# Mixture-of-experts weight ring: one whole matrix per slot instead of half matrices of two experts, a separate gather for the second pair, and the last matrices in quarters

## The reference, cut to what matters

```python
gate = p_grp * p_in / jnp.sum(p_in, axis=-1, keepdims=True)      # weights of the token's two experts
expert = grp[:, None] * MOE_PER_GROUP + top_i                    # their numbers, 0..31
...
def expert_block(args):                                          # the tokens of one expert
    x_blk, e = args
    return (jax.nn.silu(x_blk @ w_gate[e]) * (x_blk @ w_up[e])) @ w_down[e]
...
y = jax.ops.segment_sum(yb.astype(f32) * slot_w[:, None], slot_tok, num_segments=T + 1)[:T]
```

## Time and profile before

| | |
|---|---|
| median of 3 runs | 1164.86 us (1161.91 to 1165.02) |
| the profiled execution, its own time | 1167.04 us |
| its span in the trace | 1165.3 us |
| TensorE busy | 1062.5 us, 91% |
| VectorE busy | 399.1 us, 34% |
| ScalarE busy | 169.0 us, 15% |
| read from HBM | 300.47 MB |

### The profile page before, as it was taken

How to read it: one execution, slowest core, us unless ns; L and a number is a source line. 1 busy time by engine, 2 the same in 40 slices (tenths; PEclk the granted TensorE clock), 3 DMA queues, 4 the chain that set the end, 5 groups by cost and what they waited for, 6 DMA issues and landing times.

```text
span 1165.3 us, 15871 instructions
## 1 busy us (share of the span) xinstructions
PE 1062.5 (91%) x6537; PEld 588.5 (51%) x6537; DVE 399.1 (34%) x753; ACT 169.0 (15%) x361; POOL 29.7 (3%) x88
## 2 busy tenths in 40 slices
PE   5999989798999999989977979999989988898886
PEld 4777877537666666468655363333323322222222
DVE  3857642404222222330024155352323222222221
ACT  1131330301000000010045010100100100000001
POOL 5400000000000000000000000000000000000000
PEclk9999965798999999999989979999999999899999
DMA  9442000064766666654420257999999999999993
GB/s 358 179 149 74 3 2 0 9 280 178 303 276 273 277 275 276 286 224 156 167 104 1 85 204 289 368 420 420 420 419 420 420 420 421 419 420 421 420 422 125
DMA packets 39801, 302.50 MB, mean 260 GB/s; under 512 B 7578, under 2 KB 7736, under 8 KB 8632
## 3 DMA queue, kind: packets, MB, share of 16 engines
q1 hardware_dynamic: 38268, 301.29, 63.4%
q10 hardware_dynamic: 1468, 0.24, 0.1%
HBM read 300.47 MB, written 1.05 MB: 259 GB/s over the span
## 4 chain that ended last, share of the span: by engine, by line
PE 64%; SPq 23%; DVE 6%; DMA 3%; ACT 2%; issue 2%; DVEq 0%
SPq L528 22%; PE PS L1035 11%; PE PS L1610 10%; PE PS L1405 9%; PE PS L1419 9%; PE PS L1030 8%; DMA slot<-in_moe_w_up_dram 2%; PE PS L1592 2%; PE PS L1262 2%; PE PS L1567 1%; PE PS L1204 1%; PE PS L1251 1%; PE PS L1510 1%; SPq L551 1%; DVE AR L2050 1%
## 5 line engine op out<-in xcount | busy, mean ns | idle before, releaser
L1610 PE MATMUL PS<-slot,ATT 128*32 128x512 f32 (+1 forms) x1184 | 139.6, 609 | 24.5 <-DMA slot<-in_moe_w_up_dram 13.3
L1405 PE MATMUL PS<-XH,slot 128*128 128x256 f32 x512 | 111.6, 379 | 0.0
L1419 PE MATMUL PS<-slot,AR 128*128 128x512 f32 x256 | 111.2, 592 | 0.0
L1405 PEld LDWEIGHTS PS<-XH,slot 128*128 128x128 f32 x512 | 97.3, 190 | 16.2 <-issue 3.4
L1610 PEld LDWEIGHTS PS<-slot,ATT 128*32 128x32 f32 (+1 forms) x1184 | 40.1, 113 | 122.8 <-issue 106.8
L1030 PE MATMUL PS<-XH,slot 128*128 128x256 f32 x432 | 97.2, 389 | 3.5 <-DVE XH L1731 2.5
L1030 PEld LDWEIGHTS PS<-XH,slot 128*128 128x128 f32 x432 | 84.1, 195 | 16.1 <-DVE XH L1731 2.7
L1610 PE MATMUL PS<-AR,ATT 128*32 128x512 f32 (+1 forms) x608 | 71.8, 593 | 7.1 <-DMA AR<-in_moe_w_gate_dram 4.4
L1419 PEld LDWEIGHTS PS<-slot,AR 128*128 128x128 f32 x256 | 48.6, 190 | 58.2 <-issue 57.9
L1610 PE MATMUL PS<-slot,MASKS 128*32 128x512 f32 (+1 forms) x608 | 70.8, 594 | 1.0 <-DVE AR L2266 1.0
L1035 PE MATMUL PS<-slot,XH 128*128 128x256 f32 (+4 forms) x224 | 70.8, 475 | 0.0
(11 more groups left out here) (405 smaller groups left out, 992.7 us busy)
## 6 DMA issues: line engine op xcount, KB each, us to landing
slot<-in_moe_w_up_dram SPq DMA_DIRECT2D x40, 1024.0 KB, 25.6
slot<-in_moe_w_down_dram SPq DMA_DIRECT2D x40, 1024.0 KB, 25.6
slot<-in_moe_w_gate_dram SPq DMA_DIRECT2D x36, 1024.0 KB, 25.1
slot<-in_w_ffn_dram SPq DMA_DIRECT2D x16, 2048.0 KB, 9.8
AR<-in_ada_w_dram SPq DMA_DIRECT2D x16, 1536.0 KB, 11.2
AR<-in_moe_w_gate_dram SPq DMA_DIRECT2D x22, 1024.0 KB, 24.2
AR<-in_moe_w_up_dram SPq DMA_DIRECT2D x18, 1024.0 KB, 25.6
AR<-in_moe_w_down_dram SPq DMA_DIRECT2D x18, 1024.0 KB, 26.0
```

What stands on the lines that cost most here:

```text
L1405: ins = pe.matmul(PS[:, 2 * j + f // 2, (f % 2) * T:(f % 2 + 1) * T], slots[s][:, c * 512 + f * P:c * 512 + (f + 1) * P], HT[:, c, :], sta ...
L1419: ins = pe.matmul(PS[:, 4 + 2 * i + n, :], AT[:, j, f * T + i * P:f * T + (i + 1) * P], slots[s][:, f * D + n * 512:f * D + (n + 1) * 512] ...
L1610: ins = pe.matmul(PS[r0:r1, bank_, :], src[:, r0:r1], w[:, k * HALF + at:k * HALF + at + 512], start=start, stop=stop)
```

## The change

**Units.** A unit is now one whole matrix of one expert: one transfer of 2 MiB with 16 KiB per partition (`matrix`, `ring`). Units 0 and 1 are the gate matrices of the two experts of pair 0, 2 and 3 the up matrices, 4 and 5 the down matrices. TensorE waits for both units of a kind (`matrices`) and releases both at the end of the whole product. `WHICH` replaces `SIDE` and holds expert numbers.

**Gathers.** Pair 1 gets its tokens by a second `first_gather`, placed behind the up product of pair 0 (`own_selection`, `own_tokens`). The wide gather comes later in two parts: chunks 0 to 3 behind the up product of pair 1, chunks 4 to 7 behind its down product. Only pair 2 is the first to take its tokens from `HSS`. The loop of TensorE is now pairs 2 to 11 in two rounds of five; pairs 12 to 15 are written out.

**The last pair.** The scatter products of pair 14 stand ahead of the up product of pair 15. Its two down matrices come in eight transfers of 512 KiB, in quarters of the hidden dimension, with 4 KiB per partition. The down product takes a quarter at a time, and VectorE scales the first 512 output columns while TensorE makes the second (`down_first`, `yb_first`).

`YB`, the scaled output, moves to another buffer. The list of the experts with more tokens than fit loses its pair and side numbers.

The core of the diff:

```diff
-            def ring(u, g=0, sides=(0, 1)):
-                kind, half = u % UP // 2, u % 2
-                for k in range(2):
-                    sp.dma_start(RING[u % NR][:, k * HALF:(k + 1) * HALF], pair_side(kind, half, PERIOD * g + u // UP, sides[k]))\
-                        .then_inc(ring_loaded[u % NR], 16)
+            def matrix(kind, e):
+                return kinds[kind][bass.ds(e, 1)].rearrange("e p n -> p (e n)")
+            def ring(u, e):
+                sp.dma_start(RING[u % NR], matrix(u % UP // 2, e)).then_inc(ring_loaded[u % NR], 16)
...
-                sp.wait_ge(sems[released[before % UP]], PERIOD * g + before // UP + 1)
+                sp.wait_ge(sems[released[before % UP // 2]], PERIOD * g + before // UP + 1)
...
+            for f in range(4):
+                for k in range(2):
+                    sp.dma_start(RING[4 + k][:, f * D:(f + 1) * D], matrix(2, experts[k])[:, f * D:(f + 1) * D])\
+                        .then_inc(part_loaded[f], 16)
...
             pe.wait_ge(sems["first_low"], 1)
-            project(0, 0, 0, ("gate_half", "gate_filled"), EQUAL)
-            project(0, 0, 1, ("up_half", "up_filled"), EQUAL)
-            pe.wait_ge(sems["sels_ready"], 1)
-            gather()
+            w = matrices(0, 0, 0)
+            project(w, 0, EQUAL, (0, 4))
+            pe.wait_ge(sems["hs_ready"], 1)
+            project(w, 0, EQUAL, (4, KC)).then_inc(sems["gate_filled"], 1)
+            project(matrices(0, 0, 1), 1, EQUAL).then_inc(sems["up_filled"], 1)
+            pe.wait_ge(sems["sel_ready"], 2)
+            first_gather()
             pe.wait_ge(sems["am_ready"], 1)
             turn_hidden(4)
             pe.wait_ge(sems["selw_ready"], 1)
             turn_weights()
-            pe.wait_ge(sems["hss_filled"], KC)
+            w = matrices(0, 0, 2)
+            pe.wait_ge(sems["first_low"], 2)
+            pe.wait_ge(sems["hs_ready"], 2)
             pe.wait_ge(sems["ac_ready"], 1)
-            project_back(0, 0, EQUAL)
+            project_back(w, EQUAL).then_inc(sems["down_filled"], 1)
...
+            pair_in(0, 1)
+            pe.wait_ge(sems["sels_ready"], 1)
+            gather(0, 4)
+            pair_turn(0, 1)
+            pe.wait_ge(sems["hss_filled"], 4)
+            pair_out(0, 1)
+            pe.wait_ge(sems["yb_ready"], 2)
+            gather(4, KC)
...
+            pe.wait_ge(sems["hss_filled"], KC)
...
+            project(matrices(g, i, 0), 0, SKEWED).then_inc(sems["gate_filled"], 1)
+            pe.wait_ge(sems["yb_ready"], m)
+            pe.wait_ge(sems["gt_ready"], m)
             scatter(0)
-            scatter(1).then_inc(sems["x_done"], 1)
+            scatter(1)
+            project(matrices(g, i, 1), 1, SKEWED).then_inc(sems["up_filled"], 1)
+            pe.wait_ge(sems["selw_ready"], m + 1)
+            pe.wait_ge(sems["am_ready"], m + 1)
+            turn_hidden(4)
+            turn_weights()
...
+            for f in range(4):
+                pe.wait_ge(part_loaded[f], 32)
+                for n in range(2):
+                    ins = product(6 + n, SKEWED, w, f * D + n * 512, AC[:, f, :], f == 0, f == 3)
+                    if f == 3:
+                        ins.then_inc(sems[("down_first", "down_filled")[n]], 1)
...
+            own_tokens(0)
             expert_copies(0, EFF)
+            own_tokens(1)
             expert_transposed(0, EFF)
+            expert_copies(1, EFF)
+            expert_transposed(1, EFF)
             act.wait_ge(sems["place_ready"], 1)
             act.wait_ge(sems["hss_filled"], KC)
-            expert_tokens(1)
-            with act.Fori(1, NP - 1) as m:
+            expert_tokens(2)
+            with act.Fori(2, NP - 1) as m:
```

More of the change, by code:

```diff
@@ L1559, in first_gather, with gather @@
                         ins.then_inc(sems["first_gathered"], 1)
-            def gather():
-                for c in range(KC):
+            def gather(c0, c1):
+                for c in range(c0, c1):
                     if c >= 2:
@@ L1634, in _, with matrices, project @@
-            project(0, 0, 0, ("gate_half", "gate_filled"), EQUAL)
-            project(0, 0, 1, ("up_half", "up_filled"), EQUAL)
-            pe.wait_ge(sems["sels_ready"], 1)
-            gather()
+            def matrices(g, i, kind):
+                return [loaded(g, UP * i + 2 * kind + k) for k in range(2)]
+            def project(w, kind, tiles, chunks=(0, KC)):
+                for c in range(*chunks):
+                    ins = product(4 + kind, tiles, w, c * EFF, HS[:, c, :], c == 0, c == KC - 1)
+                return ins
@@ new lines, in _, with pair @@
+            pair_in(0, 1)
[6 more added lines that the diff above has]
+            gather(4, KC)
+            def pair(g, i):
+                pair_in(g, i)
+                pair_turn(g, i)
+                pair_out(g, i)
+            pe.wait_ge(sems["hss_filled"], KC)
+            rounds = (NP - 2) // PERIOD
+            with pe.Fori(0, rounds) as g:
+                for i in range(2, PERIOD + 2):
+                    pair(g, i)
@@ new lines, in _ @@
+            m = NP - 1
+            for i in range(2, m - PERIOD * rounds):
+                pair(rounds, i)
+            g, i = rounds, m - PERIOD * rounds
+            pe.wait_ge(sems["hs_ready"], m + 1)
+            project(matrices(g, i, 0), 0, SKEWED).then_inc(sems["gate_filled"], 1)
+            pe.wait_ge(sems["yb_ready"], m)
+            pe.wait_ge(sems["gt_ready"], m)
+            scatter(0)
+            scatter(1)
+            project(matrices(g, i, 1), 1, SKEWED).then_inc(sems["up_filled"], 1)
@@ L1672, in _ @@
+            pe.wait_ge(sems["gt_ready"], NP)
+            for n in range(2):
+                pe.wait_ge(sems[("yb_first", "yb_ready")[n]], (1, NP)[n])
+                for i in range(NT):
+                    ins = scatter_bank(i, n)
+            ins.then_inc(sems["x_done"], 1)
             pe.wait_ge(sems["over_ready"], 1)
@@ L2269, in _ @@
             silu_times_up(0, EFF)
-            for c in range(KC):
-                dve.wait_ge(sems["gathered"], c + 1 if c < 6 else KC)
-                if c == 6:
-                    dve.memset(HSS_END, 0.0)
-                sorted_tokens(c)
+            own_tokens(1)
             next_weights(0)
@@ L2277, in _ @@
             silu_times_up(1, EFF)
+            for c in range(4):
+                dve.wait_ge(sems["gathered"], c + 1)
+                sorted_tokens(c)
             next_weights(1)
+            expert_out(1)
+            dve.memset(HSS_END, 0.0)
+            for c in range(4, KC):
+                dve.wait_ge(sems["gathered"], c + 1 if c < 6 else KC)
+                sorted_tokens(c)
+            silu_times_up(2, EFF)
+            next_weights(2)
             further_experts()
-            expert_out(1)
-            with dve.Fori(2, NE // 2 - 1) as m:
+            expert_out(2)
+            with dve.Fori(3, NP - 1) as m:
                 silu_times_up(m, EFF)
```

177 lines of the change are left out of this document (87 added, 90 removed).

## The result

| | median | lowest to highest | runs |
|---|---|---|---|
| before | 1163.66 us | 1156.74 to 1166.97 | 10 |
| changed | 1168.87 us | 1164.99 to 1173.71 | 10 |

The ratio is 1.0057, with a 95% interval of 1.0031 to 1.0082: the change makes the kernel slower, by 0.6%. The prediction was 2 us more, and a difference too small to be told from none. It had the sign and the mechanism; that the difference can't be told did not hold, since the interval lies clear of 1.

The account below looks back on a forecast made before the run. The prediction took the arrival of the experts' matrices as the bound. Last gate units 1.1 us later plus end 0.9 us later made 2.0 us, forecast 1167 us on the median's scale, range 1160 to 1174.

Parts of the forecast that it names:

- What bounds the kernel, and the path of the loss: Experts: matrix arrival at 420 GB/s sets the time, 30.0 us a pair; TensorE needs less, 25.5 us.
- Start and second small gather: Pairs 0 and 1: first release 3.5 us later, units 14 and 15 issued at 724.7, 8.5 us pause gone but for 0.8.
- The new pauses: Stream ahead of units 20 and 22: pauses of 3.2 and 12.2 us, with 4.2 us wait and 2.2 us slower clock.
- Pace: Main stream of matrices: rows of 16 KiB go at 429.7 GB/s, 4.88 us a unit, bounds 4.87 and 4.99.
- the packet rule of the Trainium skill: Main stream: fixed cost per packet makes only 0.6%, pace 4.96 us, end 5.6 us later than the sum; chance 0.05.
- The rest of 5.4 us for the slowest engine: Last gate units: 5.4 us from the mean of the 16 DMA engines to the slowest's last landing, kept unchanged.
- End: From the last gate units' arrival: TensorE without pause, 39.5 us against 38.6, so 0.9 us later; quarters cost nothing.
- Sum: Whole kernel: 1.1 us at the last gate units plus 0.9 at the end, 2.0 us later, within measurement error.
- The pace that doesn't rise: Main stream stays at 420 GB/s whatever its row length: end 7.7 us later still, 1174.7; chance 0.17.
- The clock falls more: Pair 2's whole product is slow (7.07 us more, not 2.2), or another in the last pair: 1170.5 to 1172; chance 0.08.
- It is faster: End of stream: engines' rest shrinks to 2 us and the clock holds, 3.4 + 2.2 us earlier, 1161; chance 0.15.
- The full effect: Pair 2 starts without wait, unit 20 in time: saved 8.5 us pause and 7.7 us pace both count, about 1153; chance 0.03.

Follow-up runs that it names:

- e1: Changed kernel with the whole wide gather ahead of pair 1's down product: 468.6 us from first small gather to end of span (changed 474.9), ratio to before 0.9960.
- e9: Changed kernel with four extra products in the wait ahead of pair 2's gate: 472.3 us from first small gather to end (changed 474.9), ratio to before 1.0006.
- e2: Changed kernel with each unit but the last two in two transfers with 8 KiB rows: 479.8 us from first small gather to end, ratio to before 1.0058.
- e4: Changed kernel with the last two down matrices whole, not in quarters: 474.9 us from first small gather to end, ratio to before 1.0033.
- e3: Changed kernel with the last pair made like the others: 479.0 us from first small gather to end (changed 474.9), ratio to before 1.0050.
- e5: Changed kernel with the gathers of before, wide gather in pair 0, no second small one: 472.3 us from first small gather to end, ratio to before 0.9990.

## Why the prediction was right, and where it missed

*What bounds the kernel, and the path of the loss.* Right. e1 and e9 move the restart of the stream and leave its bytes alone, and the stretch follows. For e1 the sum gives 85.5 - (69.7 + 2 x 4.91) = 6.0 us, since unit 20 is the one that comes late there, and 6.3 were measured; for e9 2.6 and 2.6.

*Start and second small gather.* Right within 0.5 us: unit 14 was predicted 31.3 us after the small gather and issued at 30.8; the pause of 8.5 us was gone.

*The new pauses.* Right within 1.0 us: units 20 and 22 predicted at 63.8 and 85.8 us, issued at 62.8 and 85.5. The wait ahead of pair 2 was 4.5 us (4.2 predicted), the clock's share 2.6 (2.2 predicted, e9).

*Pace.* Direction right, size too large: 427 GB/s and not 429.7, so 4.91 us a unit and 70 x 0.03 = 2.1 us more than in the sum. The bursts of the earlier trace rows were 13 and 14 us long, and the sustained rate lay under their lowest. The estimate that the prediction works out from the packet rule of the Trainium skill ("DMA: Bandwidth & Descriptors", "Why small descriptors are slow (HBM only)") was 0.6% for the step from 8 to 16 KiB; e2 against the changed kernel shows 420 against 427, 1.7%. The measurement lies between that estimate and the 2.3% of my rows, nearer to the rows. The prediction also said from where on the pace decides, under about 427 GB/s, and the pace came out just there.

*The rest of 5.4 us for the slowest engine.* 435.6 - (85.5 + 1.6 + 343.8) = 4.7 us, so 0.7 less.

*End.* 39.3 us, 39.5 predicted; the quarters are worth nothing, as costed (e4). Two things stood differently: the gate product of pair 15 did not wait for its matrices, because pair 14's up product was slow (8.54 us) and TensorE became free just as they landed; and the order of the last pair is worth 4.3 us and not 2.5 within the new units (e3), since the plain order falls into the slower clock.

*Sum.* 2.0 us predicted and 3.0 in the stretch: the step that was mis-sized is the pace, by 2.1 us, against 0.7 and 0.2 the other way and 0.3 at the pauses. Whether it counts as slower was then a matter of the measurement. The interval of the changed kernel is 3.6 to 9.5 us on 1163.66, that of e4 with the same stretch 1.5 to 6.3. The stretch of 3.0 lies in the second and just under the first. Both are clear of zero, so the forecast that the difference can't be told was wrong: the sum was 1 us short, and the interval, 3 us to either side, was narrower than the 3.5 us that the prediction allowed. What the medians show beyond 3 us stays open. The start of the small gather doesn't explain it: it was at 693.4 before and between 687.8 and 697.4 in the eleven profiles with the new units, 692.7 in the mean. The medians of the unchanged kernel in the four sets of runs were 1163.66 here and 1166.39, 1164.84 and 1166.79 beside the experiments, so part of it may be this set's own. That 1168.9 lies so near the predicted 1167 is also luck in part: the prediction counted from 1164.86, and this set's median before was 1.2 us lower.

*The rivals.* The pace that doesn't rise was wrong (e2). "The clock falls more" was partly right in kind: besides pair 2 it falls in pair 7, behind the loop's jump back, and in pairs 11, 12 and 14, but there it costs tenths at most. "It is faster" needed the engines' rest to shrink from 5.4 to 2 us and the clock to hold: the rest was 4.7 and the clock fell. The full effect was excluded by TensorE's sum, as argued; it needed the gather to be free, and the two other places for it that were tried, in e1 and e5, each leave one pause of 7 to 8 us.

## What to carry to other kernels

In this ring the pause was not removed by moving the work that causes it to where the ring is just as empty; where the transfers set the pace, look for the last restart of the stream and sum from there. Splitting a job puts its tail, here the copies by two other engines, in front of whoever needs it first; keep another product behind the job, as e1 does, and the tail and the fall of the clock are both hidden. Changing the unit of a ring changes several things at once (row length, first release, length of each wait), and each has its own price and sign.

## What the runs showed of the hardware

Rows of 16 KiB in transfers of 2 MiB went at 427 GB/s and rows of 8 KiB in transfers of 1 MiB at 420, over more than 300 us, with the same bytes, order and buffers (e2).

In the twelve profiles TensorE waited 2.5 to 3.1 us ahead of 41 gate or up products of the main part. Behind 30 of these waits the product was slow (8.4 to 8.8 us in place of 7.07), behind 11 it was not, and the two kinds lie side by side in length. The same pairs were hit again in the repeats: pairs 11, 12 and 14 in both profiles of the changed kernel, 9, 11 and 13 in both of e1's. Behind shorter waits, up to 2.47 us, none was slow; the units of half matrices in the kernel before gave waits of up to 1.4 us. All 20 idle stretches of 3.7 to 4.5 us ahead of such a product had a slow one behind them, the two of the kernel before among them.

The parts of a unit do not land evenly: in the main part of eleven of the twelve profiles two or three units have a last part 0.8 to 1.9 us behind the one before it, and in e5 this moved the end.
